# Sparse attention of the second block: the mask added by an identity product, maximum and exponentials read from PSUM

## What is computed

```
q = rope(q) * hd ** -0.5                       # hd = 64, so 0.125
s = einsum(q, k)
pr = softmax(where(valid, s, -1e30), axis=-1)
o = einsum(pr, v)
o_nsa = gate_c * o_cmp + gate_s * o_slc + gate_w * o_win
```

## Time and profile before

| what | value |
|---|---|
| median of 3 runs | 1833.7 us (1832.84, 1833.70, 1835.09) |
| span of the profiled execution | 1835.8 us |
| the profiled execution's own time | not given apart from its span |
| PE, DVE, ACT, POOL busy | 1599.5, 785.5, 778.1, 968.8 us |
| attention pipeline, layer 0 | about 864 to 948 us of the span |
| attention pipeline, layer 1 | about 1403 to 1488 us |
| prologue of the second block | about 744 to 752 us |

### The profile page before, as it was taken

The page is one execution under the profiler, slowest core; times in us unless marked ns, Lnnn a source line. Parts: engine busy times, 40 slices in busy tenths (PEclk is TensorE's granted clock), DMA queues, the critical chain, the costliest instruction groups (busy, mean ns, idle before and its releaser), DMA issues. The chain is left out here.

```text
span 1835.8 us, 22140 instructions
## 1 busy us (share of the span) xinstructions
PE 1599.5 (87%) x8104; PEld 1309.1 (71%) x8104; DVE 785.5 (43%) x1135; ACT 778.1 (42%) x1233; POOL 968.8 (53%) x416
## 2 busy tenths in 40 slices
PE   5998999969989999797878789999797868889997
PEld 3876787758867877575568668887575658767885
DVE  5106853541068535108676461111127685551112
ACT  4443664334436643355531234443355522234442
POOL 4785457748854587472000339877670000358875
PEclk8999999989999999797868889999798869789999
DMA  5564335445633354551200326654651100336553
GB/s 165 160 199 121 92 110 160 155 123 162 195 115 92 113 164 146 174 174 51 92 1 1 115 69 190 181 163 144 184 155 61 58 1 22 94 104 193 167 179 125
DMA packets 120671, 228.17 MB, mean 124 GB/s; under 512 B 9968, under 2 KB 22896, under 8 KB 120560
## 3 DMA queue, kind: packets, MB, share of 16 engines
q1 hardware_dynamic: 119408, 222.51, 40.9%
q10 hardware_dynamic: 1152, 4.19, 0.8%
HBM read 225.63 MB, written 1.05 MB: 123 GB/s over the span
## 5 line engine op out<-in xcount | busy, mean ns | idle before, releaser
L162 POOL TENSOR_TENSOR parts<-raw,parts 128x1024 fp32r<-128x1024 f32 (+4 forms) x412 | 968.6, 2362 | 848.6 <-ACT parts L155 846.6
L193 PE MATMUL ps<-parts,xT 128*128 128x512 f32 (+3 forms) x2624 | 812.3, 390 | 24.3 <-ACT xT L1645 7.0
L155 ACT CAST parts<-raw 128x1024 fp32r<-128x1024 f32 (+4 forms) x412 | 417.1, 1015 | 506.7 <-PE ps L193 277.7
L193 PEld LDWEIGHTS ps<-parts,xT 128*128 128x128 f32 x2624 | 496.0, 192 | 134.0 <-ACT xT L1645 7.9
L193 PE MATMUL ps<-parts,x_low 128*128 128x512 f32 (+2 forms) x672 | 255.4, 389 | 0.0
L193 PE MATMUL ps<-parts,M_low 128*128 128x512 f32 (+2 forms) x640 | 244.9, 387 | 0.0
L193 PEld LDWEIGHTS ps<-parts,x_low 128*128 128x128 f32 x672 | 131.1, 195 | 25.2
L193 PEld LDWEIGHTS ps<-parts,M_low 128*128 128x128 f32 x640 | 120.9, 189 | 21.2
L193 PE MATMUL ps<-parts,aT 128*128 128x512 f32 x352 | 109.5, 394 | 0.0
L193 PE MATMUL ps<-parts,H_low 128*128 128x512 f32 x272 | 106.1, 395 | 0.0
L765 DVE TENSOR_TENSOR acc<-H,rope1s 128x512 f32<-128x512 f32 (+1 forms) x6 | 9.6, 1599 | 192.2 <-ACT H L646 192.1
(11 more groups left out here) (310 smaller groups left out, 2003.5 us busy)
## 6 DMA issues: line engine op xcount, KB each, us to landing
raw<-in_w_in SPq DMA_DIRECT2D x168, 512.0 KB, 3.6
raw<-in_ffn_w_down SPq DMA_DIRECT2D x44, 512.0 KB, 4.2
raw<-in_ffn_w_gate SPq DMA_DIRECT2D x40, 512.0 KB, 3.8
raw<-in_ffn_w_up SPq DMA_DIRECT2D x40, 512.0 KB, 4.4
raw<-in_w_out SPq DMA_DIRECT2D x32, 512.0 KB, 3.8
raw<-in_w_branch SPq DMA_DIRECT2D x24, 512.0 KB, 4.3
raw<-in_w_mem_kv SPq DMA_DIRECT2D x16, 512.0 KB, 3.9
raw<-in_w_in SPq DMA_DIRECT2D x16, 366.0 KB, 3.2
```

The source lines that it names most:

```text
L155: self.nc.scalar.copy(self.part(i, 0)[:, 0:nk, 0:w], self.raw(i)[:, 0:nk, 0:w]).then_inc(self.hi_ready.sem, 1)
L162: self.nc.gpsimd.tensor_tensor(self.part(i, 1)[:, 0:nk, 0:w], self.raw(i)[:, 0:nk, 0:w], self.part(i, 0)[:, 0:nk, 0:w], ALU.subtract).then ...
L193: ins = pe.matmul(b[:, 0:w], a(k0 + 2 * n + c, t), self.part(i, lo_w)[:, c, 0:w], start=(opens and n == p == 0), stop=(final and p == len( ...
```

## The change

VectorE no longer writes `p`. TensorE first puts the mask into PSUM by two products of an identity matrix with the mask (two heads, one bank, each), and the four score products then add to it. The factor 0.125 moves to the copy of the queries. VectorE takes the maximum from PSUM, and ScalarE's exponentials read PSUM and write `sm`. With `sc_read` gone, `scores(a)` waits for `E("p")` of a, which is the last exponential of group a-1. VectorE's wait for `pt_full` (the slot of `sm` is free) moves to ScalarE. Identity and masks are rounded to float32r once, by three copies on VectorE in the prologue of the second block, behind a wait for all six constants (96 on `c_in`). `cmpb` moves into the prologue's scope, and `cbias_r` lies over `cbias`.

```diff
@@ second_prologue, VectorE
             lane.done(nc.vector.memset(chip.vfirst[:, :, :], 0.0))
+            dve.wait_ge(c_in.sem, 96)
+            lane.done(nc.vector.tensor_copy(chip.ident_r[:, :], chip.ident[:, :]))
+            lane.done(nc.vector.tensor_copy(chip.cbias_r[:, :, :], chip.cbias[:, :, :]))
+            lane.done(nc.vector.tensor_copy(chip.cmpb_r[:, :, :], chip.cmpb[:, :, :]))
             dve.wait_ge(s_sq.sem, NT)
@@ TensorE, scores(a)
                     if a >= 1:
-                        pe.wait_ge(E("sc_read").sem, a)
+                        pe.wait_ge(E("p").sem, a)
...
+                    bias = (chip.cmpb_r if kind == "c" else chip.cbias_r)[:, t, 0:keys(a)].unsqueeze(1).to_broadcast([P, 2, keys(a)])
+                    for pair in (0, 2):
+                        pe.matmul(scb[:, pair:pair + 2, 0:keys(a)], chip.ident_r[:, :], bias, start=True, stop=False)
                     for s in (0, 2, 1, 3):
...
-                                        start=True, stop=True)
+                                        start=False, stop=s % 2 == 1)
@@ ScalarE
-                    TP.empty(lane, sc.copy(qT[:, 2 * i:2 * i + 2, :], turned(b)), ("q", i))
+                    TP.empty(lane, sc.activation(qT[:, 2 * i:2 * i + 2, :], turned(b), ACT.Copy, scale=0.125), ("q", i))
...
                         act.wait_ge(E("mx").sem, a + 1)
+                        if a >= 2:
+                            act.wait_ge(E("pt_full").sem, a - 1)
                         for s in range(4):
-                            p = sm[:, a % 2, s, 0:keys(a)]
-                            lane.done(sc.activation(p, p, ACT.Exp, bias=nmx[:, a, s:s + 1], accum_out=den[:, a, s:s + 1]),
-                                      E("p") if s == 3 else None)
+                            lane.done(sc.activation(sm[:, a % 2, s, 0:keys(a)], scb[:, s, 0:keys(a)], ACT.Exp, bias=nmx[:, a, s:s + 1],
+                                                    accum_out=den[:, a, s:s + 1]), E("p") if s == 3 else None)
@@ VectorE
                         dve.wait_ge(E("sc_full").sem, k + 1)
-                        if k >= 2:
-
-                            dve.wait_ge(E("pt_full").sem, k - 1)
-                        p = sm[:, k % 2, :, 0:nk]
-                        bias = (chip.cmpb if kind == "c" else chip.cbias)[:, t, 0:nk].unsqueeze(1).to_broadcast([P, 4, nk])
-                        stt(p, scb[:, :, 0:nk], 0.125, bias, ALU.mult, ALU.add, E("sc_read"))
                         lane.settle()
-                        lane.done(v.tensor_reduce(nmx[:, k, :], p, AX_X, ALU.max, negate=True), E("mx"))
+                        lane.done(v.tensor_reduce(nmx[:, k, :], scb[:, :, 0:nk], AX_X, ALU.max, negate=True), E("mx"))
```

More of the change, by code:

```diff
@@ L281, in __init__ @@
     def __init__(self, ctx, nc):
+        place = Places(ctx, nc)
         def sb(name, shape, dtype=F32):
+            if dtype == F32:
+                return place(name, shape)
             return ctx.enter_context(nc.sbuf_tensor(name, shape, dtype))
@@ L290, in __init__ @@
         self.cbias = sb("cbias", [P, NT, S])
+        self.cbias_r = place.over("cbias_rounded", "cbias", [P, NT, S])
         self.ps = ctx.enter_context(nc.psum_tensor("ps", [P, 8, HALF], F32))
@@ L941, in second_prologue @@
         junk = ctx.enter_context(nc.sbuf_tensor("fin_junk", [P, D], F32))
+        chip.cmpb = ctx.enter_context(nc.sbuf_tensor("cmpb", [P, NT, P], F32))
         ss = ctx.enter_context(nc.sbuf_tensor("fin_ss", [P, 3, NT], F32))
@@ L2202, in build @@
         chip.rope2 = sb("rope2s", [P, NT, 2, HD])
-        chip.cmpb = sb("cmpb", [P, NT, P])
+        chip.cmpb_r = ctx.enter_context(nc.sbuf_tensor("cmpb_rounded", [P, NT, P], F32R))
+        chip.ident_r = ctx.enter_context(nc.sbuf_tensor("ident_rounded", [P, P], F32R))
         chip.rowv = sb("rowv", [P, NT])
```

## The result

The changed kernel takes 1854.1 us (median of 4 runs, 1851.3 to 1857.8), the kernel before 1833.3 us beside it (4 runs): ratio 1.0111, 95% interval 1.0086 to 1.0135. Run once more in a later sitting it took 1849.4 us against 1831.1, ratio 1.0104 (1.0085 to 1.0123). So it is slower by 18 to 21 us; forecast were 15.3, within 10 to 22. Ratios and intervals here are those on record; they are not the quotient of the two medians beside them, from which they differ by about 0.1% at most.

A forecast was written before the change was run, and what follows sets the result against it. Large products fill most of the span; in the pipeline TensorE bounds the front, a chain through VectorE the back. 5.5 + 2 x (5.4 - 2 + 1.5) = 15.3 us on 1833.7 gives 1849.0 us, range 1839 to 1860.

The forecast's parts named there:

- The waits that were named: Front: TensorE waits for ScalarE's exponentials ahead of the mask products, for about 1, 3 and 2 us.
- Term 1, the ring: Front, k=1 to 4: mask, scores, compression, transposes, copy and exponentials become a closed ring each k; +5.4 us a layer.
- Term 2, the mask products: Mask products on TensorE: 0.46 us a group with 256 keys, about 0.24 with 128, counted within the front.
- the rival with the float32 pace: Mask products run at plain float32 pace, 11 us a layer more on TensorE; about 1868 us; chance 0.04.
- Term 3, the back: Back, k=5 to 13: VectorE loses one pass a group; -2 us a layer, bounds -6.2 and +4.
- Term 4, the clock: Front: gaps let TensorE's clock drop to the lower level; +1.5 us a layer, between 0 and 4.7.
- the clock rival: Clock falls at each k of the front, three drops a layer; 27.3 us more, 1861.0 us; chance 0.12.
- its strict reading: Front: idling or transposing for 4 to 5 us of each 9 drops TensorE's clock in every k; sum 1861.0 us.
- One sign that I had named: Front of the changed profile: scores(4) comes some 25 us after scores(1), instead of 17.
- Term 5, reads from PSUM: Maximum and exponentials read PSUM instead of SBUF: both put at 0, bounds +1.2 and -2.9 us in all.
- Term 6, the prologue: Second block's prologue, once: VectorE waits for all constants, then makes three copies; +5.5 us.

The follow-up runs named there:

- Experiment 4: Kernel before with one edit: scores wait for the last exponential of the previous group instead of VectorE's first pass; 1849.3 us, ratio 1.0073.
- experiment 5: Kernel before, with the compression products of k = 1 to 4 placed ahead of the scores; 1833.1 us against 1833.4, ratio 0.9999.
- experiment 2: Changed kernel, with the compression products of k = 1 to 4 placed ahead of mask and scores; 1841.9 us, ratio 1.0048.
- experiment 7: Changed kernel plus twelve products nobody reads in TensorE's gap at the end of k=2; 1853.6 us, ratio 1.0108; second sitting 1847.6 us, ratio 1.0081.
- experiment 8: Changed kernel with compression first, casts late and two score tiles for groups of 128 keys; 1831.3 us against 1833.4, ratio 0.9994.
- Experiment 6: Changed kernel without the mask products, so nothing is masked and the score products start the accumulation; 1840.2 us, ratio 1.0036.
- experiment 1: Changed kernel with two casts ahead of any wait, the wait for constants and third cast behind the passes over `x`; 1850.2 us, ratio 1.0082.
- experiment 9: Kernel of experiment 8 plus products nobody reads, 11 at the end of k=6 and 12 at the end of k=12; 1829.3 us against 1831.1, ratio 0.9999.

## Why the prediction was right, and where it was off

**The sign, and the mechanism: right.** Experiment 4 puts the wait alone into the kernel before and gets 15 us of the loss; experiment 5 shows that the order by itself is worth nothing; experiment 2 takes the wait out of the front's way and gets 12 us back. The waits that were named (about 1, 3 and 2 us) are 1.22, 3.08 and 2.10. The time lies nearer to the forecast than the stages do (18 to 21 us, where the stages add up to 21.5, against 15.3): part of that nearness is luck.

**Term 1, the ring: right, bar the masks.** From mask to mask it was to take 6.8, 9.3 and 8.7 us, then 4.7 to the exponentials of group 4. At the full clock it takes 6.96, 9.44 and 8.89 (this one from experiment 7). For the last step the rows give 4.98: 0.44 to the scores (909.16 to 909.60), 0.65 to the compression, 1.85 for it (893.68 to 895.53 in the kernel before), 2.04 from the transposes (913.74) to the exponential (915.78). That is 30.3 us for 29.5 predicted.

**Term 2, the mask products: mis-sized.** I took the pace of a long row of products, 0.228 us for 512 columns, and got 0.24 and 0.46 a group. A pair takes 0.43 and 0.66, about 0.2 more in either case; the single product of experiment 8, of 512 columns, takes 0.41, the same 0.2 over its columns. The twelve of experiment 7 take 0.25 each. I read this as 0.2 us paid once, where a short group of products meets products of another kind (that it is the meeting was not tested); the rate itself was right, and the rival with the float32 pace is out. It adds 0.8 us to each front, and term 3 pays it too. I also held the masks for cheap in the back, where about half of the groups were to pay. Experiment 6 takes 12 to 14 us off for 24 groups, as much as if nearly all of them were on the path, though its profile does not separate masks from clock.

**Term 3, the back: the number near, its place wrong.** -2 was forecast, -1.2, -1.3, -2.2 and -2.7 are measured, -1.9 on average. But groups 9 to 11 were to give all of it, 0.7 us each, and the groups ahead of them nothing, and the traces show the reverse. From the start of the back to the maximum of group 8 it takes 23.8 and 24.3 us before, and 22.4, 21.9, 22.7 and 22.7 in the four changed pipelines: 1.7 less. From there to the maximum of group 11 it takes 15.2 before, and 15.7, 16.5, 14.4 and 14.4 after: on average nothing. So that the number fits is luck. The removed passes do free VectorE there, but it then waits for TensorE's `values`, which stand behind the wait for the exponentials, the mask and the scores: 3.5 us between the maxima of groups 8 and 11 in layer 0 (1.92, 0.16 and 1.42), where it waited 0.56 before. The prediction also read VectorE as busy without a gap there; these 0.56 us were idle. The rest of the spread goes with the clock: ten pipelines have the changed kernel's order in the back (experiments 1 and 7 included), and it takes 43.5 or 43.6 us in the four with a mean clock of 0.88 and 44.2 to 44.9 in the six with 0.77 to 0.79.

**Term 4, the clock: the term that was mis-sized most.** +1.5 us a layer was taken, 0 to 4.7 allowed. The four fronts give, for k=3, 11.76, 10.45, 10.44 and 10.43 us from mask to mask, against 8.89: 1.9 on average. For k=4 they give 6.62, 6.47, 8.06 and 8.03, up to the exponentials of group 4, against 4.98: 2.3. So 4.2 us a layer. I had let the clock fall once, and partly; it falls twice, at k=3 and at k=4. It doesn't fall at every k, as the clock rival had it: at k=2, with a gap of 1.22 us and transposes before it, it stays up in all four. The Trainium skill (TensorE: Matmul & The Clock Gate, Part 4) says that transposes don't count as activity; its strict reading gave three drops and 7.5 us, the trace shows two and 4.2. One sign that I had named shows it at once: scores(4) were to come 25 us after scores(1), and their masks are 28.2 us apart in layer 0 (881.00 to 909.16) and 26.8 in both layers of the second profile.

**Term 5, reads from PSUM: right at 0 for VectorE, a small gain for ScalarE.** Groups by shape in the changed kernel (columns as in the earlier trace rows):

```profile
L1910 DVE TENSOR_REDUCE nmx<-ps 128x4 f32<-128x512 f32 x16 | 11.1, 692 | 9.0 <-PE ps L1289 7.0 <-DVE KK L1705 0.9
L1910 DVE TENSOR_REDUCE nmx<-ps 128x4 f32<-128x1024 f32 x8 | 9.8, 1225 | 28.1 <-PE ps L1289 27.9
...
L1601 ACT ACTIVATE arena<-ps,nmx 128x128 f32<-128x128 f32 x64 | 22.7, 370 | 10.8 <-DVE nmx L1910 10.8
```

The maximum takes 692 and 1225 ns against 686 and 1220. The Trainium skill (VectorE: DVE Perf Modes, The TRN2 errata) has a fixed part of 120 cycles for VectorE's reads from PSUM and 58 for those from SBUF. Here the difference is 5 or 6 ns, so the page's difference of 62 cycles does not show in this change. An exponential of 128 columns takes 370 ns against 390. Four of them with the reads of their sums take 1.51 us (886.39 to 887.90) against 1.65.

**Term 6, the prologue: right.** +5.1 in the two profiles, +4.9 over all kernels with these casts, for 5.5; experiment 1 takes 4.5 of it back by moving the wait.

**The sum.** With what was measured, a layer costs 5.4 (the ring) + 0.8 (start of the masks) + 4.2 (clock) - 1.9 (back) = 8.5, where the cut gives 8.2, and the prologue 5.1 (0.3 of the difference is k=0, ahead of the ring, which takes 11.5 us instead of 11.8). The forecast was 4.9 a layer and 5.5. Of the 3.6 us by which this sum is higher, 2.7 are the clock.

## What to carry to other kernels

When a producer's buffer is read by a later stage than before, its release moves, and what counts is which work stands behind the new wait on the producer's queue: here 3 us of independent products stood behind it, and one changed wait cost 15 us while 18.5 us of VectorE's work were saved. Put independent work ahead of such a wait first: that, with two casts moved ahead of the wait for the transfer and the third behind other work, brought the changed kernel back to the time of the old one. Before filling a gap with products that nobody reads, see that they stand ahead of the wait that makes the gap: behind it they are added work (about 3 us a layer in experiment 9). A mask by an identity product is not free on TensorE: price each short group of products with 0.2 us on top of its columns, and count it wherever TensorE's results are waited for.

## What the runs showed of the hardware

- A gap on TensorE can cost twice: at k=3 it is 3.08 us of waiting, and then 1.5 to 2.9 us more for the next 4.9 us of work (mask, scores and compression of k=3), part of it at 1.2 GHz; the gap of 1.22 us at k=2 brought no fall in any of the four pipelines. Products that nobody reads, put into the gap, kept the clock up behind it: for 2.4 us a layer in experiment 7, and for 2.3 us in experiment 9, up to the second lot. The later falls (k=4, and the gap of 3.17 us at the end) are there with and without the products; no run shows that filling one gap brings on another fall.
- In the same kernel the same place costs differently from one pipeline to the next (k=3: 11.76 or 10.45, k=4: 6.5 or 8.0), as the low stretch is longer or shorter: at k=3 the clock is 0.50 from 898 to 903 us and full from 905 in layer 0 of the first profile, but 0.79 from 1445 to 1448 us and full behind in layer 1, where the work of k=3 begins at 1442.7. What decides it stays open.
- Rounding 512 float32 columns to float32r on VectorE takes 0.42 us, 256 take 0.29, 128 take 0.23.
